# Scores ahead of transposes, logits ahead of low parts: a new order inside the head-pair loop of a one-core hybrid attention layer

## Chip, cores and metric

One core of one Trainium2 chip runs the whole layer in one launch. The metric is the device time of that launch in microseconds (us); lower is better. The engines are named as in the profile: PE (TensorE, with PEld for its weight loads), DVE (VectorE), ACT (ScalarE), POOL (GpSimd) and SP (SyncE, which here only issues DMAs). They run separate instruction queues, each in its own written order, and meet through semaphores.

## What is computed

One decoder layer for a sequence of 256 tokens and a model width of 1024, in float32. The input is RMS-normed and projected to two head groups of 8 heads with 64 columns each. Group A is attention with forget gates: a bias of cumulated log gates is added to the causal logits. Group B is block-sparse attention with a distance bias; with 256 tokens there is one block, so it is plain causal attention with that bias. Every head's output is multiplied by a SiLU gate; the 16 heads' outputs are projected back to 1024 columns, RMS-normed and added to the input.

```python
h = rms_norm(x, norm_pre_g)
q_a, k_a, v_a, g_a, f_a, q_b, k_b, v_b, g_b = split(h @ w_in)
logits_a = q_a @ k_a.T / 8 + F[t] - F[s]          # F = cumsum(log_sigmoid(f_a + b)), causal
logits_b = q_b @ k_b.T / 8 - slope * (t - s)       # causal
y_a = softmax(logits_a) @ v_a * silu(g_a)
y_b = softmax(logits_b) @ v_b * silu(g_b)
out = x + rms_norm(concat(y_a, y_b) @ w_out, norm_post_g)
```

## The kernel before

Every float32 product is made of parts. A matrix is split into a high part (ACT copies it to a rounded type) and a low part (DVE subtracts the high part from the original), and a product is three matmuls: high by high, low by high, high by low.

The weights come in units of 128 x 1024 floats. SP loads them one after the other into a ring of four slots (`raw`); ACT makes the high part of a unit (line 369), DVE the low part (line 570, `next_low`), and the slot is free for the next load when the low part is done. Units of values and gates come first. From unit `QK_0` on, units alternate: `query_unit(i)`, `key_unit(i)` for the head pairs i = 0 to 7 (pairs 0 to 3 are group A, 4 to 7 group B), and behind them the second half of the output weights.

The attention part is a loop written out by hand, with one head pair in each of several stages. In turn i (i = 2 to 7) PE runs `query(i)` and `key(i)`, 24 matmuls each at line 850, `scores(i - 1)` at line 944, `transposes(i - 2)` of the probabilities at lines 951 to 953 and `values(i - 2)` at lines 961 to 966. The other engines do in a turn, in the order of their queues:

- ACT: high part of query i (482); high parts of the transposed probabilities of i-2 (457, 458); high part of the weights of key i+1 (369); high part of y of i-3 (471, from turn 3 on); the four exponentials of i-1 with their row sums (465); high part of key i (486); high part of the weights of query i+2 (369); the upper half of the value result of i-2, `y_cross` (477).
- DVE: `query_low(i)` (719); `probs_low(i - 2, 0)` and `(i - 2, 1)` (695), the low parts of the transposed probabilities, with `row_logits(i - 1)` (709), four reductions that add the bias and find the row maximum, between them; the low part of the weights of key i+1 (570); `row_inverses(i - 1)` (715); `key_low(i)` (724); the low part of the weights of query i+2 (570); `gated(i - 2)` (730, 735), which sums y and multiplies it with its gate.
- POOL: `norm_probs(i - 1)`, two multiplications of the probabilities by the inverse row sums (324); the bias of pair i, two operations (310 and 311 for group A, 318 for group B); the low part of y of i-2 (330).

What waits for what, where the change touches it: `scores(i - 1)` needs the high and low parts of query and key i-1, and that `row_logits(i - 2)` has read the bank. `transposes(i - 2)` needs `norm_probs(i - 2)`. `row_logits(i - 1)` needs the scores and both bias operations of pair i-1. `values(i - 2)` needs both `probs_low(i - 2, ...)`. `query(i)` and `key(i)` need the low part of their weights. The bias operations of pair i wait for `row_logits(i - 1)`.

Ahead of the loop DVE also makes the low parts of the weights of `key_unit(2)` and `query_unit(3)`. Behind it comes a tail in which PE fills its waits with the first parts of the output projection (`out_part`, line 1011): out parts, `transposes(6)`, `scores(7)`, out parts, `values(6)`, out parts, `transposes(7)`, out parts, `values(7)`, and the rest of the projection. In the tail ACT's queue holds the high part of y of pair 5 ahead of the high parts of the transposed probabilities of pair 6, and DVE's holds `gated(5)`, `probs_low(6, 0)`, `row_logits(7)`, `probs_low(6, 1)`. The change does not touch the tail's order.

Of the kernel before, what the change touches and what calls it, by code (L numbers as in the profile page):

```python
# [62 lines left out]
def hybrid_layer(nc, xt, x, g_pre, w_units, w_f, f_bias, w_out, g_post, out):  # L63
# [5 lines left out]
    def sem(name):  # L69
        return ctx.enter_context(nc.semaphore(name))  # L70

    with ctx:
# [103 lines left out]
        s_logits = sem("logits_ready")  # L176
# [382 lines left out]
        def _(dve):  # L559
# [8 lines left out]
            def unit_low(s, count, width=UNIT):  # L568
                dve.wait_ge(s_hi, count)
                nc.vector.tensor_tensor(w[1][:, s, 0:width], raw[:, s, 0:width], w[0][:, s, 0:width].bitcast(F32),  # L570
                                        ALU.subtract).then_inc(s_lo, 1)
# [120 lines left out]
            def probs_low(i, n):  # L692
                dst, src = ((p_t0, pt0_ps), (p_t1, pt1_ps))[n]
                dve.wait_ge(s_pthi, 2 * i + n + 1)
                nc.vector.tensor_tensor(dst[1][:, :, :], src, dst[0][:, :, :].bitcast(F32),  # L695
                                        ALU.subtract).then_inc(s_ptlo, 1)

            def row_logits(i):
                dve.wait_ge(s_qk, i + 1)
                dve.wait_ge(s_bias, 2 * i + 2)  # L700
                for a in range(2):
                    if i < FOX_PAIRS:
                        biases = bias[:, a, 0:P], decay[:, 2 * i + a, :]
                    else:
                        biases = bias[:, a, P:SEQ], bias[:, a, :]
                    for t, (lo, hi) in enumerate(((0, P), (P, NB))):
                        c = 2 * a + t

                        nc.vector.tensor_tensor_reduce(out=logits[:, a, lo:hi], in0=s_ps[a][:, lo:hi], in1=biases[t],  # L709
                                                       scale=-SCALE, scalar=3.0e38, op0=ALU.add, op1=ALU.min,  # L710
                                                       accum_out=neg_max[:, c:c + 1]).then_inc(s_logits, 1)

            def row_inverses(i):
                dve.wait_ge(s_exp, 4 * i + 4)
                nc.vector.reciprocal(row_inv[:, :], row_sum[:, :]).then_inc(s_inv, 1)  # L715

            def query_low(i, b):
                dve.wait_ge(s_qhi, i + 1)
                nc.vector.tensor_tensor(q[1][:, b, :], bank[0][:, 0:SEQ], q[0][:, b, :].bitcast(F32),
                                        ALU.subtract).then_inc(s_qlo, 1)  # L720
# [16 lines left out]
            def next_low(u):  # L737

                unit_low(u % RING, u + 1)

            def query_unit(i):

                return QK_0 + 2 * i

            def key_unit(i):

                return QK_0 + 2 * i + 1
# [11 lines left out]
            row_inverses(0)  # L759
            key_low(1)  # L760
            next_low(key_unit(2))
            next_low(query_unit(3))

            dve.wait_ge(s_gate, 1)
            for i in range(2, PAIRS):
                if i > 2:
                    dve.wait_ge(s_norm, 2 * i - 2)
                query_low(i, i % 2)
                probs_low(i - 2, 0)
                row_logits(i - 1)  # L770
                probs_low(i - 2, 1)
                next_low(key_unit(i + 1))
                row_inverses(i - 1)
                key_low(i)
                next_low(query_unit(i + 2))
                gated(i - 2)
# [64 lines left out]
        def _(pe):  # L841
# [94 lines left out]
            def scores(i, b):  # L936
                pe.wait_ge(s_qhi, i + 1)
                pe.wait_ge(s_qlo, i + 1)
                pe.wait_ge(s_khi, i + 1)
                pe.wait_ge(s_klo, i + 1)  # L940
                for t, (lo, hi) in enumerate(((0, P), (P, NB))):
                    for n, (x, z) in enumerate(PASSES):
                        for a, own in enumerate(head_rows):
                            last = nc.tensor.matmul(s_ps[a][:, lo:hi], q[x][own, b, t * P:(t + 1) * P],  # L944
                                                    k[z][own, 0:hi - lo], start=n == 0, stop=n == len(PASSES) - 1)
                last.then_inc(s_qk, 1)
# [22 lines left out]
            def query(i, b, halfway=None):  # L969
                pe.wait_ge(s_lo, QK_0 + 1 + 2 * i)  # L970
                column_unit(bank[0], 2 * b, h, halfway)

            def key(i, b):
                pe.wait_ge(s_lo, QK_0 + 2 + 2 * i)
                column_unit(bank[1], 2 * b + 1, h)
# [11 lines left out]
            def attend(i, b, first=False):  # L987
                pe.wait_ge(s_qlo, i)
                query(i, b)
                if not first:  # L990
                    pe.wait_ge(s_ptlo, 2 * i - 4)
                transposes(i - 2)
                pe.wait_ge(s_logits, 4 * i - 4)
                scores(i - 1, 1 - b)
                key(i, b)
                if not first:
                    pe.wait_ge(s_ysum, 2 * i - 4)
                values(i - 2)
# [93 lines left out]
```

## Time and profile before

| | |
|---|---|
| Median of 3 runs | 147.05 us (146.78 to 147.18) |
| The profiled execution: time, span | 147.58 us, 145.8 us |
| PE matmul busy | 137.5 us, 94% |
| PEld busy | 129.0 us, 88% |
| DVE busy | 110.8 us, 76% |
| ACT busy | 99.6 us, 68% |
| POOL busy | 44.7 us, 31% |
| Granted TensorE clock, mean over the span | 0.992 |

The time of the profiled execution holds 1.78 us outside its span. All times of the trace count from the start of the span. The loop runs from 63.4 us (first matmul of `query(2)`) to 112.97 us, the tail from there on. A row of the timeline gives start and duration; durations of neighbours on one engine overlap a little, so the distance between two starts is what an instruction takes from its engine. "x2" in a row of PE's scores means the two heads of the pair, which use different halves of the array's rows.

### The profile page before, as it was taken

Reading aid. Unit: us, or ns where it says so; the run is one execution under the profiler, and the core shown is the slowest. Engines: PE = TensorE matmul, PEld = TensorE weight load, DVE = VectorE, ACT = ScalarE, POOL = GpSimd, SP = SyncE. Lnnn points to the kernel's source line nnn. Section 1 sums busy time; section 2 is a strip of 40 time slices with the busy share of each in tenths; the row PEclk is TensorE's granted clock in tenths of the full one; section 3 lists DMA queues with packets and bytes.
Section 4 is the critical chain, followed back from the end, with each engine's and each line's share of the span. In section 5 each row is a group of like instructions: output and inputs, shape, how many; then the busy total and the mean of one; then the engine's idle time right before and its main releaser. Section 6 shows DMA issues by size and latency. Waiting matters only on the chain.

```text
span 145.8 us, 2904 instructions
## 1 busy us (share of the span) xinstructions
PE 137.5 (94%) x1076; PEld 129.0 (88%) x1076; DVE 110.8 (76%) x243; ACT 99.6 (68%) x209; POOL 44.7 (31%) x70
## 2 busy tenths in 40 slices
PE   7999999999999999999999999999999999999920
PEld 7899899999999999998899999999999888898910
DVE  0384965999999996679989898989899866240891
ACT  4466989488957488598568788795959495244530
POOL 2621100000000012019293755465472924200241
PEclk9999999999999999999999999999999999999996
DMA  4899997488876999941744443525174000000034
GB/s 90 268 323 396 400 389 296 127 334 241 288 214 216 323 378 406 368 161 18 270 148 144 146 144 103 189 66 216 27 246 173 0 0 4 0 0 0 0 144 144
DMA packets 9725, 26.96 MB, mean 185 GB/s; under 512 B 1384, under 2 KB 2416, under 8 KB 9456
## 3 DMA queue, kind: packets, MB, share of 16 engines
q1 hardware_dynamic: 9120, 25.57, 50.7%
q10 hardware_dynamic: 592, 1.22, 2.5%
q8 instruction: 8, 0.13, 0.4%
q14 instruction: 5, 0.04, 0.1%
HBM read 25.73 MB, written 1.06 MB: 184 GB/s over the span
## 4 chain that ended last, share of the span: by engine, by line
PE 43%; DVE 24%; DMA 15%; ACT 6%; issue 4%; SPq 3%; POOL 2%; POOLq 1%; ACTq 0%; DVEq 0%
PE bank L850 20%; PE bank L1011 13%; DVE w_lo L570 11%; DMA h<-in_x 6%; DMA raw_out<-in_w_out 5%; DMA raw<-in_w_units 4%; PE bank L944 4%; DVE h L614 2%; DVE v L628 2%; DVE gate L635 2%; SPq L207 2%; DVE h_lo L641 2%; DVE wo_lo L646 2%; PE bank L961 1%; ACT w_hi L369 1%
## 5 line engine op out<-in xcount | busy, mean ns | idle before, releaser
L570 DVE TENSOR_TENSOR w_lo<-raw,w_hi 128x1024 fp32r<-128x1024 f32 (+1 forms) x33 | 44.2, 1343 | 8.4 <-ACT w_hi L369 8.4
L369 ACT ACTIVATE w_hi<-raw 128x1024 fp32r<-128x1024 f32 (+1 forms) x33 | 34.5, 1057 | 6.4 <-DMA raw<-in_w_units 4.6
L850 PE MATMUL bank<-h_hi,w_hi 128*128 128x256 f32 x128 | 36.7, 286 | 0.0
L850 PE MATMUL bank<-h_hi,w_lo 128*128 128x256 f32 x128 | 35.6, 278 | 0.0
L850 PE MATMUL bank<-h_lo,w_hi 128*128 128x256 f32 x128 | 35.6, 278 | 0.0
L850 PEld LDWEIGHTS bank<-h_hi,w_hi 128*128 128x128 f32 x128 | 24.1, 188 | 0.9
L850 PEld LDWEIGHTS bank<-h_hi,w_lo 128*128 128x128 f32 x128 | 24.0, 188 | 0.0
L850 PEld LDWEIGHTS bank<-h_lo,w_hi 128*128 128x128 f32 x128 | 24.0, 188 | 0.0
L324 POOL TENSOR_TENSOR probs<-probs,row_inv 128x256 f32<-128x256 f32 (+1 forms) x16 | 12.9, 828 | 23.0 <-DVE row_inv L715 23.0
L850 PE MATMUL bank<-xg_hi,w_hi 128*128 128x256 f32 x64 | 17.9, 280 | 0.0
L310 POOL TENSOR_TENSOR bias<-squares,causal 128x256 f32<-128x256 f32 x4 | 6.2, 1548 | 37.7 <-DMA squares<-decay_rows_scratch 37.7
L850 PE MATMUL bank<-xg_lo,w_hi 128*128 128x256 f32 x64 | 17.7, 277 | 0.0
L850 PE MATMUL bank<-xg_hi,w_lo 128*128 128x256 f32 x64 | 17.7, 276 | 0.0
L465 ACT ACTIVATE probs<-logits,neg_max 128x128 f32<-128x128 f32 (+1 forms) x32 | 14.2, 447 | 2.4 <-DVE neg_max L709 2.3
L850 PEld LDWEIGHTS bank<-xg_hi,w_hi 128*128 128x128 f32 x64 | 12.0, 188 | 0.1
L850 PEld LDWEIGHTS bank<-xg_lo,w_hi 128*128 128x128 f32 x64 | 12.0, 188 | 0.0
L850 PEld LDWEIGHTS bank<-xg_hi,w_lo 128*128 128x128 f32 x64 | 12.0, 188 | 0.0
L695 DVE TENSOR_TENSOR p_t_lo<-bank,p_t_hi 128x512 fp32r<-128x512 f32 (+1 forms) x16 | 8.7, 550 | 3.2 <-ACT p_t_hi L457 3.0
L860 PE MATMUL bank<-w_hi,xg_hi 128*128 128x256 f32 (+2 forms) x50 | 10.4, 330 | 0.3 <-ACT w_hi L400 0.3
L860 PE MATMUL bank<-w_hi,xg_lo 128*128 128x256 f32 (+2 forms) x50 | 9.9, 320 | 0.0
L860 PE MATMUL bank<-w_lo,xg_hi 128*128 128x256 f32 (+2 forms) x50 | 9.9, 319 | 0.0
L730 DVE TENSOR_TENSOR y_sum<-bank,y_cross 64x256 f32<-64x256 f32 x16 | 6.6, 413 | 3.7 <-ACT y_cross L477 3.4
(131 smaller groups left out, 318.5 us busy)
## 6 DMA issues: line engine op xcount, KB each, us to landing
raw<-in_w_units SPq DMA_DIRECT2D x30, 512.0 KB, 5.4
raw_out<-in_w_out SPq DMA_DIRECT2D x4, 512.0 KB, 6.6
raw<-in_w_out SPq DMA_DIRECT2D x4, 512.0 KB, 3.4
h<-in_x SPq DMA_DIRECT2D x2, 512.0 KB, 8.0
squares<-decay_rows_scratch ACTq DMA_DIRECT2D x1, 1024.0 KB, 7.9
x_t<-in_x SPq DMA_DIRECT2D x1, 1024.0 KB, 7.6
raw<-in_w_units SPq DMA_DIRECT2D x3, 256.0 KB, 4.8
out<-x_t SPq DMA_DIRECT2D x3, 256.0 KB, 2.0
```

Source lines behind the costliest of these rows:

```text
L207: sp.dma_start(raw[:, u % RING, lo:hi].rearrange("p (a c) -> p a c", a=n), w_units[units, :, part][0:n].rearrange("a p c -> p a c")).then_ ...
L310: pool.tensor_tensor(bias[:, :, 0:P], decay[:, heads, 0:P], mask, ALU.add).then_inc(s_bias, 1)
L324: pool.tensor_tensor(probs[:, :, lo:hi], probs[:, :, lo:hi], row_inv[:, t::2].unsqueeze(2).to_broadcast((P, 2, hi - lo)), ALU.mult).then_i ...
L369: nc.scalar.activation(w[0][:, s, 0:width], raw[:, s, 0:width], ACT.Copy).then_inc(s_hi, 1)
L465: nc.scalar.activation(probs[:, a, lo:hi], logits[:, a, lo:hi], ACT.Exp, bias=neg_max[:, c:c + 1], scale=-1.0, accum_out=row_sum[:, c:c + ...
L570: nc.vector.tensor_tensor(w[1][:, s, 0:width], raw[:, s, 0:width], w[0][:, s, 0:width].bitcast(F32), ALU.subtract).then_inc(s_lo, 1)
L695: nc.vector.tensor_tensor(dst[1][:, :, :], src, dst[0][:, :, :].bitcast(F32), ALU.subtract).then_inc(s_ptlo, 1)
L730: nc.vector.tensor_tensor(y_sum[own, :], pv_ps[head_rows[0], a, :], y_cross[own, :], ALU.add).then_inc(s_ysum, 1)
L850: last = nc.tensor.matmul(dst, stationary(a, j), moving(b, j), start=n == 1, stop=n == count * len(PASSES))
L860: last = nc.tensor.matmul(v_banks[t][c][:, lo - first:hi - first], xg[a][:, u, t * P:(t + 1) * P], w[b][:, u % RING, lo:hi], start=u == 0 ...
L944: last = nc.tensor.matmul(s_ps[a][:, lo:hi], q[x][own, b, t * P:(t + 1) * P], k[z][own, 0:hi - lo], start=n == 0, stop=n == len(PASSES) - 1)
L1011: last = nc.tensor.matmul(dst, y[a][:, p, t * P:(t + 1) * P], wide, start=p == 0 and (a, b) == PASSES[0], stop=p == PAIRS - 1 and (a, b) = ...
```

## The change

Two queues get another order. On PE, each turn of the loop runs query, scores, transposes, key, values; before, the transposes stood ahead of the scores. On DVE, each turn runs `row_logits(i - 1)` ahead of `probs_low(i - 2, 0)`, no longer between the two `probs_low`. And the low part of the weights of `query_unit(3)`, which stood ahead of the loop, is made in turn 2, behind `probs_low(0, 1)` and ahead of the low part of `key_unit(3)`. No instruction is added or removed, and the queues of ACT, POOL and SP are as before.

```diff
             key_low(1)
             next_low(key_unit(2))
-            next_low(query_unit(3))
 
             dve.wait_ge(s_gate, 1)
             for i in range(2, PAIRS):
                 if i > 2:
                     dve.wait_ge(s_norm, 2 * i - 2)
                 query_low(i, i % 2)
+                row_logits(i - 1)
                 probs_low(i - 2, 0)
-                row_logits(i - 1)
                 probs_low(i - 2, 1)
+                if i == 2:
+                    next_low(query_unit(3))
                 next_low(key_unit(i + 1))
                 row_inverses(i - 1)
                 key_low(i)
...
             def attend(i, b, first=False):
                 pe.wait_ge(s_qlo, i)
                 query(i, b)
+                pe.wait_ge(s_logits, 4 * i - 4)
+                scores(i - 1, 1 - b)
                 if not first:
                     pe.wait_ge(s_ptlo, 2 * i - 4)
                 transposes(i - 2)
-                pe.wait_ge(s_logits, 4 * i - 4)
-                scores(i - 1, 1 - b)
                 key(i, b)
```

## Rows read from the trace of the kernel before

**Rows 1.** Chain that ended last, in order of time (start, us, what).

```profile
67.68 1.75 DVE w_lo L570
```

**Rows 2.** Timeline of PE, turn 2 and its end (start, us, instruction, count, idle before).

```profile
66.24 0.28 PE L850 MATMUL bank<-h_hi,w_lo 128*128 128x256 f32 x1
66.73 0.33 PE L951 MATMUL bank<-ident,probs 128*128 128x128 f32 x1 [0.21 <-POOL probs L324]
...
67.33 0.27 PE L953 MATMUL bank<-ident,probs 128*128 128x128 f32 x1
67.53 0.33 PE L944 MATMUL bank<-k_hi,q_hi 64*128 64x128 f32 x2
...
68.21 0.28 PE L944 MATMUL bank<-k_hi,q_lo 64*128 64x256 f32 x2
68.42 0.39 PE L850 MATMUL bank<-h_hi,w_hi 128*128 128x256 f32 x1
...
71.23 0.28 PE L850 MATMUL bank<-h_hi,w_lo 128*128 128x256 f32 x1
71.85 0.39 PE L961 MATMUL bank<-p_t_hi,v 128*128 128x256 f32 x1 [0.34 <-DVE p_t_lo L695]
...
72.67 0.33 PE L850 MATMUL bank<-h_hi,w_hi 128*128 128x256 f32 x1
```

**Rows 3.** Timeline of PE: the first matmul of `values(1)`, `(5)` and `(6)`.

```profile
80.01 0.28 PE L961 MATMUL bank<-p_t_hi,v 128*128 128x256 f32 x1
...
112.25 0.28 PE L961 MATMUL bank<-p_t_hi,v 128*128 128x256 f32 x1
...
120.30 0.28 PE L961 MATMUL bank<-p_t_hi,v 128*128 128x256 f32 x1
```

**Rows 4.** Timeline of DVE, tail.

```profile
119.57 0.42 DVE L695 TENSOR_TENSOR p_t_lo<-bank,p_t_hi 128x256 fp32r<-128x256 f32 x1
```

**Rows 5.** Timeline of DVE, turn 2.

```profile
65.96 1.80 DVE L570 TENSOR_TENSOR w_lo<-raw,w_hi 128x1024 fp32r<-128x1024 f32 x1 [0.53 <-ACT w_hi L369]
...
69.35 0.41 DVE L719 TENSOR_TENSOR q_lo<-bank,q_hi 128x256 fp32r<-128x256 f32 x1
69.68 0.67 DVE L695 TENSOR_TENSOR p_t_lo<-bank,p_t_hi 128x512 fp32r<-128x512 f32 x1
70.28 0.28 DVE L709 CUSTOM_DVE_ANT_0 logits<-bank,bias 128x128 f32<-128x128 f32 x1
...
71.39 0.41 DVE L695 TENSOR_TENSOR p_t_lo<-bank,p_t_hi 128x256 fp32r<-128x256 f32 x1
71.72 1.21 DVE L570 TENSOR_TENSOR w_lo<-raw,w_hi 128x1024 fp32r<-128x1024 f32 x1
...
73.11 0.42 DVE L724 TENSOR_TENSOR k_lo<-bank,k_hi 128x256 fp32r<-128x256 f32 x1
```

**Rows 6.** Timeline of ACT, turn 7 and the start of the tail.

```profile
108.55 0.60 ACT L457 ACTIVATE p_t_hi<-bank 128x512 fp32r<-128x512 f32 x1 [0.27 <-PE bank L953]
...
112.73 1.05 ACT L369 ACTIVATE w_hi<-raw 128x1024 fp32r<-128x1024 f32 x1
...
116.79 0.42 ACT L471 ACTIVATE xg_hi<-y 128x256 fp32r<-128x256 f32 x1 [2.19 <-DVE y L735]
```

**Rows 7.** Timeline of POOL, turns 2 and 3.

```profile
66.63 1.71 POOL L310 TENSOR_TENSOR bias<-squares,causal 128x256 f32<-128x256 f32 x1
68.31 1.72 POOL L311 TENSOR_TENSOR squares<-squares,causal 128x256 f32<-128x256 f32 x1
73.10 1.61 POOL L324 TENSOR_TENSOR probs<-probs,row_inv 128x256 f32<-128x256 f32 x2 [3.07 <-DVE row_inv L715]
74.67 1.71 POOL L310 TENSOR_TENSOR bias<-squares,causal 128x256 f32<-128x256 f32 x1
76.34 0.74 POOL L311 TENSOR_TENSOR squares<-squares,causal 128x256 f32<-128x256 f32 x1
```

**Rows 8.** The page's sixth part: loads of weight units (KB each, median us to landing).

```profile
raw<-in_w_units SPq DMA_DIRECT2D x30, 512.0 KB, 5.4
```

## The prediction

> **What bounds the kernel now.** I read the page first: PE's matmuls are busy 94% of the span, no other engine over 76% (the table of the profile above). That says PE, but a share over the whole span does not say what a reordering is worth. So I went to the chain of work that ended last. From the values of turn 2 (71.85) to the end of the projection it is PE alone; ahead of that it runs for some us through DVE, and the low part of `query_unit(3)`, 1.75 us, is its largest piece there [rows 1]. Then PE's timeline shows what turn 2 loses. Matmuls of 256 columns follow each other every 0.11 to 0.12 us. Two gaps are wider: 66.24 to 66.73, where the transposes wait for POOL's normed probabilities (0.38 lost), and 71.23 to 71.85, where the values wait for DVE (0.50 lost) [rows 2]. A matmul behind a wait is also longer, 0.33 for 0.27 and 0.39 for 0.28: its weight load is not hidden, 0.06 and 0.11. Together 1.05 us. From turn 3 on PE never waits: `values(1)` at 80.01 and `values(5)` at 112.25 lie four times 8.06 apart [rows 3].
>
> The reader should see one thing more, which the chain does not show: how near behind PE the others run. In the tail `probs_low(6, 1)` starts at 119.57 and takes 0.42 [rows 4]; with the 0.05 that lay between such an end and PE in turn 2 (71.39 + 0.41 to 71.85) `values(6)` could have started at 120.04, and it started at 120.30 [rows 2, 3, 5]. The slack is 0.26 us. What makes `probs_low(6, 1)` so late is a relay: transposes(5), ACT from the transposed probabilities (108.55) to the weights (112.73) and, past DVE's `gated(5)`, to y (116.79) [rows 6], then `probs_high(6)`, DVE's low part, logits, low part.
>
> **Part 1, PE's order.** In turn 2 the scores fill the wait. `scores(1)` starts 0.20 behind the query's last matmul, as it does behind the transposes (67.33 to 67.53), at 66.44; it lasts 0.68 to its last start (67.12). The transposes then start at 67.33 if this step costs what scores to key cost, 0.21, and the last of them at 67.93 (before at 67.33, with the scores still to come). The key follows at 68.04 instead of 68.42 [rows 2]. Its first load would be hidden again (0.11). A gain of 0.49 for PE here.
>
> In every other turn no wait is filled and five steps between blocks are only dealt out anew: query to transposes (0.11), transposes to scores (0.20), scores to key (0.21 + 0.11) become query to scores (0.20), scores to transposes, transposes to key (0.11 by the nearest case, matmuls that follow each other). Scores to transposes the trace does not show. From below it is 0.11, a plain step; from above 0.32, as scores to key with the exposed load. I take 0.27, with the 0.06 that a transpose showed behind a wait: PE's turn changes by -0.05, next to nothing. With the ends it is -0.2 to 0 a turn.
>
> But in each turn the transposes come later, by the scores in front of them: 0.20 - 0.11 + 0.68 + 0.27 = 1.04 us.
>
> **Part 2, DVE's order and the moved low part.** `query_low(2)` no longer stands behind `query_unit(3)` and starts at 67.68 instead of 69.35. `row_logits(1)` follows at 68.02, but it needs the bias of pair 1. POOL's two operations took 1.71 and 1.72 us; the same at 76.34 took 0.74 [rows 7]. The long ones each start just before a DVE subtraction of a unit: DVE's own, issued at 65.96, takes 1.80 where one beside an idle POOL takes 1.21 [rows 5]. They take turns. DVE has the first turn until 67.68, POOL's first operation runs to 68.31, and the second, with DVE's subtraction gone, ends at 68.31 + 0.74 = 69.05. So logits start at 69.08, 1.06 late, and DVE stands. They take 1.11 (70.28 to 71.39), `probs_low(0, 0)` 0.60, `(0, 1)` 0.42: `values(0)` at 71.25, not 71.85 [rows 2, 5].
>
> The Trainium skill says of this, in "SBUF — State Buffer", section "SBUF: two separate sides", that VectorE with two SBUF inputs and GpSimd hold a shared port pair for a whole instruction and the other blocks; these rows agree. By a split of bandwidth instead, the split norms of the next paragraph would cost POOL some 0.5 us less and the sum would be about 0.2 lower.
>
> Now the moved subtraction is late in its turn: 71.13 to 72.34 (1.21), and `query(3)` needs it: 72.38 against 72.67 before, while PE would be ready at 71.25 + 0.82 = 72.07. Of 1.05 us in reach 0.29 are left. Behind it `key_unit(3)` takes 1.14; `key_low(2)` and `norm_probs(1)` start at 73.5 to 73.65, not at 73.1 [rows 5, 7]. And the low part of `query_unit(4)` now is issued 0.34 behind `key_low(2)`, while POOL is in the first of its two norm operations (1.61 for both), since ACT, which waited for logits before, has the high part ready. DVE gets the pair between the two: the second norm ends at about 76.1 to 76.3, and `transposes(1)`, ready at 76.15, wait up to 0.2. The biases of pair 2 end at about 77.8 to 78.1 instead of 77.08. `row_logits(2)` waits for them, and with 1.11 + 0.60 + 0.42 + 0.05 `values(1)` starts at 80.0 to 80.3. It was 80.01: the gain is gone. I take +0.1.
>
> **Part 3, the loop.** From ACT's start on the transposed probabilities to its query weights is 4.18, to the end of DVE's gated y another 4.06, then query low 0.33, logits 1.11, low parts 0.60 and 0.47: next turn's values at 10.75 us [rows 2, 5, 6]. PE used to need 3.7 from ACT's start (108.55) to the values of that turn (112.25) [rows 3, 6]; without the scores between them, 1.04, it needs 2.66, and comes to the next ones at 2.66 + 8.06 = 10.7, where it used to come 1.04 later. So cover of a microsecond is used up, and PE meets DVE at each values: 0 to 0.1 a turn, taken as 0, with the 0.05 that PE's turn gains against it.
>
> **Part 4, the tail.** Here the order is the old one, so PE comes to `values(6)` as early as before, but the relay started with `transposes(5)`, 1.04 later. `values(6)` starts at 120.04 + 1.04 + 0.1 = 121.2 and shows its load (0.11); before 120.30. That is 0.99, and behind `values(6)` only PE works until the projection ends, so it stays to the end.
>
> **DMAs.** The moved low part frees the slot for `query_unit(5)` 3 us later; ACT wants that unit two turns on, at about 81, and a load takes 5.4 us from issue to landing [rows 8]. It is hidden; without that cover it would be a load's length late.
>
> **Sum.** +1.0 us. The profiled execution becomes 148.6 from 147.58; it lay 0.53 above the median, so the median goes from 147.05 to **148.05**.
>
> **Rivals.**
> *A, faster: only PE counts.* All 1.05 us of waits go and the relay has room: 146.0. For it: PE is the whole chain from 71.85. Against it: 0.26 us of slack at `values(6)`. It decides if the relay shrinks by 0.8.
> *B, same: the front gain stays.* If POOL's second bias ends by 68.3 and the norms are not split, `query(3)` starts at 71.6 and `values(1)` about 0.9 earlier; the tail takes it back: 147.1. Against it: POOL cannot start that bias before 68.31 and needs 0.74.
> *C, slower still.* If scores to transposes costs 0.32 and the key's load is exposed too (0.11), PE loses 0.12 a turn; if DVE and POOL collide in the group B turns as well, 0.1 to 0.2 more each: 148.8.
>
> **Numbers.** Forecast (+0.45 to +1.5) 0.62, A 0.07, B 0.17, C 0.14. The bounds: steps -0.4, turn 2 from -0.5 to +0.3, loop up to +0.5. With B's half inside, the range is 147.1 to 148.8. A difference under 0.3% (0.44 us) cannot be told from none. Faster 0.07, same 0.17, slower 0.76.
>
> **What would show it.** After: scores at 66.4 with no gap; logits(1) at 69.1 with DVE idle ahead of it; `query(3)` at 72.4; POOL's second norm of pair 1 or its bias at about 1.7 to 2 us; `values(1)` at 80.0 to 80.3; turns of 8.05 to 8.15; and in the tail PE waiting 0.5 to 1 us for DVE at `values(6)`, near 121.2. If PE does not wait there, the forecast is wrong.

## The result, and the profile after

The median of 21 runs is 148.42 us (147.74 to 150.20), against 147.18 us for the kernel before (21 runs, 146.35 to 149.31). Now and then an execution of either kernel is slower as a whole, and the ratio leaves those out. It is 1.0081, with an interval of 1.0054 to 1.0108: the change costs 0.8%, or 1.19 us on 147.18. Forecast were 148.05 us and a difference of +1.0.

The profiled execution took 147.79 us, for a span of 146.0 us at a granted clock of 0.993. The page's table of engines, after:

```profile
PE 136.9 (94%) x1076; PEld 128.0 (88%) x1076; DVE 112.7 (77%) x243; ACT 99.1 (68%) x209; POOL 44.8 (31%) x70
```

As many instructions, and nearly the busy times of the table before the change. DVE alone has 1.9 us more, although it does the same work; nearly all of it, 1.8 us, is in the low parts of the weights (46.0 for 44.2), which run longer where POOL holds them up. The time is in the order, so the timelines have to tell it.

PE's timeline from the end of the query to the first values (start, us, instruction):

```profile
66.12 0.28 PE L851 MATMUL bank<-h_hi,w_lo 128*128 128x256 f32 x1
66.33 0.33 PE L945 MATMUL bank<-k_hi,q_hi 64*128 64x128 f32 x2
...
67.00 0.28 PE L945 MATMUL bank<-k_hi,q_lo 64*128 64x256 f32 x2
67.21 0.33 PE L952 MATMUL bank<-ident,probs 128*128 128x128 f32 x1
...
67.81 0.27 PE L954 MATMUL bank<-ident,probs 128*128 128x128 f32 x1
67.84 0.36 PE L851 MATMUL bank<-h_hi,w_hi 128*128 128x256 f32 x1
68.04 0.28 PE L851 MATMUL bank<-h_lo,w_hi 128*128 128x256 f32 x1
...
70.75 0.28 PE L962 MATMUL bank<-p_t_hi,v 128*128 128x256 f32 x1
```

The scores come 0.21 behind the query, with no gap, and both waits of turn 2 [rows 2] are gone: `values(0)` stands at 70.75, not at 71.85. The new step from scores to transposes is 0.21, with 0.06 of exposed load on the first transpose (0.33 for 0.27).

DVE's timeline in turns 2 and 3 (in brackets the idle time before, and what ended it):

```profile
66.92 0.42 DVE L719 TENSOR_TENSOR q_lo<-bank,q_hi 128x256 fp32r<-128x256 f32 x1 [0.61 <-ACT q_hi L482]
67.73 0.29 DVE L709 CUSTOM_DVE_ANT_0 logits<-bank,bias 128x128 f32<-128x128 f32 x1 [0.39 <-POOL squares L311]
...
72.94 2.06 DVE L570 TENSOR_TENSOR w_lo<-raw,w_hi 128x1024 fp32r<-128x1024 f32 x1 [0.41 <-ACT w_hi L369]
```

And POOL's:

```profile
63.62 1.61 POOL L324 TENSOR_TENSOR probs<-probs,row_inv 128x256 f32<-128x256 f32 x2 [9.74 <-DVE row_inv L715]
65.18 1.72 POOL L310 TENSOR_TENSOR bias<-squares,causal 128x256 f32<-128x256 f32 x1
66.86 0.73 POOL L311 TENSOR_TENSOR squares<-squares,causal 128x256 f32<-128x256 f32 x1
72.30 1.61 POOL L324 TENSOR_TENSOR probs<-probs,row_inv 128x256 f32<-128x256 f32 x2 [4.71 <-DVE row_inv L715]
```

As forecast, the second bias operation shrinks from 1.72 [rows 7] to 0.73 once DVE's subtraction is out of its way, and DVE stands ahead of the logits until that bias is there. But it stands 0.39 us, not 1.06. In turn 3 the norms of pair 1 are not split (1.61 for both); instead DVE's low part of `query_unit(4)`, 72.94, waits behind the second one and takes 2.06, where the same instruction took 1.74 before (at 74.06) and one beside an idle POOL takes 1.21 [rows 5]. `values(1)` is the first to feel it.

The later values of PE's timeline, and the tail:

```profile
79.08 0.36 PE L962 MATMUL bank<-p_t_hi,v 128*128 128x256 f32 x1 [0.15 <-DVE p_t_lo L695]
...
117.96 0.40 PE L1012 MATMUL bank<-wo_hi,xg_lo 128*128 128x512 f32 x1
118.41 0.47 PE L1012 MATMUL bank<-w_hi,xg_hi 128*128 128x512 f32 x1
118.72 0.40 PE L1012 MATMUL bank<-w_lo,xg_hi 128*128 128x512 f32 x1
...
119.64 0.40 PE L1012 MATMUL bank<-w_hi,xg_lo 128*128 128x512 f32 x1
120.37 0.36 PE L962 MATMUL bank<-p_t_hi,v 128*128 128x256 f32 x1 [0.34 <-DVE p_t_lo L695]
```

And what DVE does in front of it:

```profile
119.80 0.42 DVE L695 TENSOR_TENSOR p_t_lo<-bank,p_t_hi 128x256 fp32r<-128x256 f32 x1
```

`values(5)` is at 111.47, so from there to `values(6)` it is 8.90 us; before it was 8.05 [rows 3]. Two places on PE hold the 0.85. Matmuls of the projection follow each other every 0.23 us. The step from 117.96 to 118.41 is 0.45 and the next 0.31: 0.30 lost to the low part of y of pair 5, which POOL makes from 117.51 to 118.26. From 119.64 to 120.37 it is 0.73: 0.50 lost to `probs_low(6, 1)`. The rest, 0.05, is the turn itself. The two losses have not two causes, though: nothing that DVE does for `probs_low(6, 1)` waits for the out part of pair 5, so without the first pause PE would only have waited longer at `values(6)`.

One thing misleads in this pair of profiles: the spans differ by 0.2 us (145.8 and 146.0), the medians by 1.2. The place is ahead of the loop, in ACT's timeline, where the fourth unit of the output weights is awaited. First before, then after:

```profile
60.20 1.06 ACT L373 ACTIVATE wo_hi<-raw_out 128x1024 fp32r<-128x1024 f32 x1 [1.49 <-DMA raw_out<-in_w_out]
```
```profile
58.46 1.06 ACT L373 ACTIVATE wo_hi<-raw_out 128x1024 fp32r<-128x1024 f32 x1 [0.15 <-DMA raw_out<-in_w_out]
```

That load was late in the profiled execution of before. DVE takes the low part of this unit ahead of the inverse row sums of pair 0, and POOL's norms wait for those. They started at 63.62 after, and before at

```profile
65.06 1.61 POOL L324 TENSOR_TENSOR probs<-probs,row_inv 128x256 f32<-128x256 f32 x2 [9.35 <-DVE row_inv L715]
```

The experiments below had to find out whether the waits of turn 2 come from this.

### The profile page after: what moved, and what is told of

Its sections match the earlier page's. It is cut to its first block, busy times and chain, and to the rows that moved or that the text cites. A ratio compares the mean times of both kernels' runs of the same rounds, so it can differ in the third digit from the quotient of the medians.

```text
span 146.0 us, 2904 instructions
## 1 busy us (share of the span) xinstructions
PE 136.9 (94%) x1076; PEld 128.0 (88%) x1076; DVE 112.7 (77%) x243; ACT 99.1 (68%) x209; POOL 44.8 (31%) x70
## 3 DMA queue, kind: packets, MB, share of 16 engines
q10 hardware_dynamic: 592, 1.22, 2.2%
HBM read 25.73 MB, written 1.06 MB: 184 GB/s over the span
## 4 chain that ended last, share of the span: by engine, by line
PE 67%; DVE 9%; POOL 7%; ACT 7%; issue 4%; DMA 3%; SPq 1%; POOLq 1%; DVEq 0%
PE bank L851 34%; PE bank L861 15%; PE bank L1012 9%; DMA raw<-in_w_units 3%; DVE w_lo L570 3%; ACT probs L465 2%; PE bank L945 2%; DVE logits L709 2%; POOL bias L310 2%; POOL probs L324 2%; DVE p_t_lo L695 2%; PE bank L962 1%; ACT w_hi L369 1%; PE bank L952 1%; POOL x_t L355 1%
## 5 line engine op out<-in xcount | busy, mean ns | idle before, releaser
L570 DVE TENSOR_TENSOR w_lo<-raw,w_hi 128x1024 fp32r<-128x1024 f32 (+1 forms) x33 | 46.0, 1398 | 7.4 <-ACT w_hi L369 7.3
L861 PE MATMUL bank<-w_hi,xg_hi 128*128 128x256 f32 (+2 forms) x50 | 9.9, 319 | 1.1 <-ACT w_hi L400 1.1
L457 ACT ACTIVATE p_t_hi<-bank 128x512 fp32r<-128x512 f32 x8 | 4.8, 598 | 8.6 <-PE bank L954 8.6
L695 DVE TENSOR_TENSOR p_t_lo<-bank,p_t_hi 128x512 fp32r<-128x512 f32 (+1 forms) x16 | 8.2, 547 | 3.0 <-ACT p_t_hi L457 3.0
```

Of the source, the lines that this page charges most:

```text
L457: nc.scalar.activation(p_t0[0][:, :, :], pt0_ps, ACT.Copy).then_inc(s_pthi, 1)
L861: last = nc.tensor.matmul(v_banks[t][c][:, lo - first:hi - first], xg[a][:, u, t * P:(t + 1) * P], w[b][:, u % RING, lo:hi], start=u == 0 ...
```

## The experiments

Each ratio is to the kernel before, run on the same chip in the same rounds. Stage distances are between first matmuls of `values(i)`, written V(i), in the profiled execution:

| kernel | ratio (interval) | V0 | V0 to V1 | V1 to V5 | V5 to V6 | V0 to V7 |
|---|---|---|---|---|---|---|
| before | 1 | 71.85 | 8.16 | 32.24 | 8.05 | 55.37 |
| before, again | 1.0023 (0.9989 to 1.0057) | 71.89 | 8.17 | 32.23 | 8.05 | 55.41 |
| before, third slot | 0.9996 (0.9966 to 1.0026) | 70.86 | 8.07 | 32.23 | 8.05 | 55.27 |
| after | 1.0081 (1.0054 to 1.0108) | 70.75 | 8.33 | 32.39 | 8.90 | 56.65 |
| after, again | 1.0104 (1.0043 to 1.0164) | 70.85 | 8.33 | 32.39 | 8.88 | 56.63 |
| after, third slot | 1.0071 (1.0037 to 1.0106) | 71.06 | 8.33 | 32.38 | 8.91 | 56.65 |
| last turn in the old order | 1.0041 (1.0006 to 1.0076) | 70.98 | 8.32 | 32.39 | 8.43 | 56.12 |
| ACT's tail swapped | 1.0068 (1.0036 to 1.0100) | 71.00 | 8.93 | 32.39 | 8.37 | 56.65 |
| both of these | 1.0066 (1.0024 to 1.0107) | 70.85 | 8.32 | 32.39 | 8.42 | 56.07 |
| change in turn 2 only | 1.0010 (0.9980 to 1.0039) | 71.29 | 8.32 | 32.32 | 8.04 | 55.61 |
| PE's order only | 1.0162 (1.0111 to 1.0213) | 70.97 | 8.40 | 33.52 | 8.69 | 57.64 |
| DVE's order only | 1.0066 (1.0036 to 1.0097) | 71.22 | 9.09 | 32.23 | 8.04 | 56.34 |
| moved low part only | 1.0045 (1.0009 to 1.0081) | 70.95 | 8.82 | 32.24 | 8.05 | 56.02 |
| the same with a wait | 1.0031 (0.9992 to 1.0070) | 71.33 | 8.64 | 32.32 | 8.05 | 55.92 |

### The kernel before, again

No edit. Expected:

> The kernel before, unchanged, for a second profile of it and for the noise of a comparison. Theory (relay): in the profile of the changed kernel ACT and DVE entered the loop 1.4 us earlier than in the profile of before (first norm operation of POOL at 63.62 against 65.06), because a load of output weights landed earlier. If that differs from execution to execution, this profile can show the transposes of turn 2 without a wait, values(0) at 70.6 to 70.9 instead of 71.85, values(5) at 110.9 to 111.2, and a span near 144.8. Rival (the waits of turn 2 belong to the order of the queues): values(0) again at 71.8 to 71.9 and the span at 145.8. Time: no difference, ratio 1.000 within 0.3%.

The ratio is no different from 1, but the profiled execution had the late load again: ACT had the unit at 60.23, the norms of pair 0 started at 65.09, V(0) was at 71.89, the span 145.8. The hoped-for early execution did not come, and the question stayed open.

### A third slot for the output weights

On the kernel before: one more slot, and the fourth unit's load issued one place earlier in SP's queue, so that it lands earlier.

```diff
-OUT_BEHIND = (V_UNITS + 3, V_UNITS + 5, V_UNITS + 11, V_UNITS + 13)
+OUT_BEHIND = (V_UNITS + 3, V_UNITS + 5, V_UNITS + 11, V_UNITS + 12)
...
-        raw_out = sb("raw_out", [P, 2, UNIT])
+        raw_out = sb("raw_out", [P, 3, UNIT])
...
-                if j > 1:
-                    sp.wait_ge(s_olo, j - 1)
-                sp.dma_start(raw_out[:, j % 2, :], w_out[j]).then_inc(s_raw_out_in[j % 2], 16)
+                if j > 2:
+                    sp.wait_ge(s_olo, j - 2)
+                sp.dma_start(raw_out[:, j % 3, :], w_out[j]).then_inc(s_raw_out_in[j % 3], 16)
...
```

> The kernel before with a third staging slot for the output weights and the load of output unit 3 issued one unit load earlier; both queues in the old order. Theory: the waits of turn 2 (1.05 us in two profiles of before) come from the high part of output unit 3, for which ACT waits 1.5 us at 60.2; with an earlier landing ACT and DVE enter turn 2 over 1 us earlier, the transposes of turn 2 and values(0) do not wait, and the span is 144.8 to 145.0: ratio 0.993 to 0.998 (some executions of before are early as they are). Rival (the waits belong to the order of DVE's queue): values(0) still at 71.8, ratio 1.000.

The span is 144.7, as expected, and PE waits for nothing in the loop or in the tail. ACT's row for the unit, and PE's first matmuls of `values(0)` and `values(6)`:

```profile
58.27 1.05 ACT L373 ACTIVATE wo_hi<-raw_out 128x1024 fp32r<-128x1024 f32 x1
```
```profile
70.86 0.28 PE L961 MATMUL bank<-p_t_hi,v 128*128 128x256 f32 x1
...
119.21 0.28 PE L961 MATMUL bank<-p_t_hi,v 128*128 128x256 f32 x1
```

So the load's landing is what makes the waits of turn 2. But the ratio is 1.00, not the 0.993 to 0.998 expected. This execution took 146.52 us, and the median of before beside it was 146.65: by its time, the usual execution of before is already one without these waits, and the two profiles of before happened to be late ones. That is read from the times; no profile of the unchanged kernel before shows an early landing. With this kernel as the measure, span 144.7 against 146.0, the profiles show +1.3 us, which answers to the 1.19 of the ratio: 0.26 in turn 3 (V0 to V1), 0.16 in the four turns behind it, 0.85 from `values(5)` to `(6)`, 0.11 from there to `values(7)` (the exposed load of `values(6)` for the most part), less 0.11 by which V(0) comes earlier.

### The third slot on the kernel after, and the kernel after again

The same diff, on the kernel after:

> The changed kernel with the third staging slot and the earlier load of output unit 3, which took the waits of turn 2 out of the kernel before (span 144.7). Theory: in the change PE has no wait left in turn 2 that the landing could set, and the loss is in turn 3, the loop and the tail: values(0) at 70.7 to 70.9, values(5) to values(6) at 8.9, span 146.0, so 1.3 us over the kernel before with the same staging and ratio 1.006 to 1.009 to before. Rival (the change's loss comes with the late landing): ratio under 1.003.

And the kernel after without an edit:

> The changed kernel once more, on the chip and in the call of its repaired versions. Theory: ratio 1.007 to 1.010; a second profile, with values(5) to values(6) again at 8.9 us; if the output weights land late in it, values(0) to values(1) is near 8.9 instead of 8.33, by the norms of pair 1 being split (2.60 us) and logits(2) waiting 1 us for the bias. Rival (the first profile is not typical): a tail distance near 8.05.

Both repeat the kernel after within 0.02 us in each stage (8.33, 32.38 and 32.39, 8.91 and 8.88). With the third slot the loop as a whole began 0.3 us later (norms of pair 0 at 63.93), so V(0) and the span of 146.3 lie a little above what was expected; the ratio of the kernel after again, 1.0104 from six runs, lies a little above its 1.010. The load was early in all three, so the loss does not need a late one. What a late one adds, the swapped kernel below shows. The median of the first, 148.01, lies 1.47 above the 146.54 of the third slot on before, from another chip.

### The last turn in the old order

On the kernel after, PE runs turn 7 as before, so that `transposes(5)` are as early as they were.

```diff
                 query(i, b)
-                pe.wait_ge(s_logits, 4 * i - 4)
-                scores(i - 1, 1 - b)
+                if i < PAIRS - 1:
+                    pe.wait_ge(s_logits, 4 * i - 4)
+                    scores(i - 1, 1 - b)
...
                 transposes(i - 2)
+                if not (i < PAIRS - 1):
+                    pe.wait_ge(s_logits, 4 * i - 4)
+                    scores(i - 1, 1 - b)
                 key(i, b)
```

> The changed kernel, with PE's old order (transposes ahead of scores) in the last turn of the loop alone, turn 7. Theory (relay): the cost sits between values(5) and values(6), where the chain transposes(5), ACT, gated y, ACT, low parts, values(6) starts 1.04 us later than before. With transposes(5) early again that distance falls from 8.90 to about 8.5 us, since DVE still comes later from the turns before, and the time is 0.4 us (0.2 to 0.8) under the changed kernel: ratio to before 1.003 to 1.007. Rival 1 (each turn's steps on PE cost more in the new order): one turn of six is restored, so a sixth of 1.2 us, 0.2 us, and the distance values(5) to values(6) stays 8.9. Rival 2 (the loss is in turn 2): no change, 1.008.

V5 to V6 falls from 8.90 to 8.43, and the whole from 1.0081 to 1.0041, as expected (the two intervals overlap, so it is the stage that tells). The high part of y of pair 5 starts at 116.33, not 117.02. PE waits neither at the out part of pair 5 (118.52 to 118.75) nor at `values(6)` (119.89 to 120.12): with `transposes(5)` early the relay costs nothing, so the late transposes do drive the tail. The 0.38 that stays is no rest of it. Most of it is a new wait, 0.29 at `transposes(6)`, which the last repair below explains.

### ACT's tail swapped

On the kernel after, ACT takes the transposed probabilities of pair 6 ahead of y of pair 5.

```diff
-            y_high(PAIRS - 3)
             probs_high(PAIRS - 2)
+            y_high(PAIRS - 3)
```

> The changed kernel, with one exchange in ACT's tail: the high parts of the transposed probabilities of pair 6 are made ahead of the high part of y of pair 5, not behind it. The loop is untouched. Theory (relay): ACT waits 2.35 us for y there while the transposes have been done since 115.9; without that wait DVE is bound by its own queue, PE waits less at values(6), and the time falls by 0.5 us (0.3 to 0.9) against the changed kernel: ratio to before 1.002 to 1.006; values(5) to values(6) near 8.5 us or less. Rival 1 (cost of PE's steps or of the loop): the tail's order does not matter, ratio stays 1.008 and the distance from values(0) to values(5) stays 40.7.

V5 to V6 is 8.37: `values(6)` no longer waits for DVE, and what is left, 0.27, is lost at the out part of pair 5, which waits for POOL's low part of y (118.33 to 119.08; the matmul starts at 119.23). The ratio, expected at 1.002 to 1.006, is 1.0068 (1.0036 to 1.0100); that interval holds both the 0.5 us that the stage gained and no gain at all. The profile cannot explain the median of twelve runs, but it shows something else: this execution had the load late (59.74, not quite the 60.20 of before), and with it turn 3 cost 8.93. It is the one profile of a changed kernel in which the forecast's own premise held, so it shows what the forecast described. DVE's timeline:

```profile
73.44 1.55 DVE L570 TENSOR_TENSOR w_lo<-raw,w_hi 128x1024 fp32r<-128x1024 f32 x1
...
77.65 0.29 DVE L709 CUSTOM_DVE_ANT_0 logits<-bank,bias 128x128 f32<-128x128 f32 x1 [1.10 <-POOL squares L311]
```

POOL's and PE's:

```profile
73.29 2.60 POOL L324 TENSOR_TENSOR probs<-probs,row_inv 128x256 f32<-128x256 f32 x2 [4.71 <-DVE row_inv L715]
```
```profile
72.13 0.36 PE L851 MATMUL bank<-h_hi,w_hi 128*128 128x256 f32 x1 [0.26 <-DVE w_lo L570]
```

`query(3)` waits for the moved low part, until 72.13; DVE's subtraction is issued 0.15 behind the start of the first norm and comes between the two, which then take 2.60 for 1.61; the biases are late, DVE stands 1.10 ahead of the logits, and `values(1)` is at 79.93.

### Both repairs together

```diff
-            y_high(PAIRS - 3)
             probs_high(PAIRS - 2)
+            y_high(PAIRS - 3)
...
+                if i < PAIRS - 1:
+                    pe.wait_ge(s_logits, 4 * i - 4)
+                    scores(i - 1, 1 - b)
```

> The changed kernel with both repairs of the tail at once: PE's old order in turn 7, and ACT's high parts of the transposed probabilities of pair 6 ahead of the high part of y of pair 5. Theory (relay): each repair alone left about 0.35 of the 0.85 us between values(5) and values(6) (8.43 and 8.37, from 8.90; 8.05 before), because after the one the other still delayed; with both the distance is 8.05 to 8.10 and PE does not wait at values(6). Left are turn 3 and the loop, 0.3 to 0.6 us: ratio 1.002 to 1.004. Rival (a third cause in the tail, DVE's own lateness): 8.3 or more stays.

Missed. V5 to V6 is 8.42, no better than with either alone, and the ratio 1.0066. `values(6)` follows the projection without a gap (119.75 to 119.98). Another wait is there, at `transposes(6)`:

```profile
114.92 0.40 PE L1016 MATMUL bank<-wo_hi,xg_lo 128*128 128x512 f32 x1
115.45 0.30 PE L952 MATMUL bank<-ident,probs 128*128 128x128 f32 x1
```
```profile
112.71 2.60 POOL L324 TENSOR_TENSOR probs<-probs,row_inv 128x256 f32<-128x256 f32 x2 [1.93 <-DVE row_inv L715]
```
```profile
113.11 1.30 DVE L570 TENSOR_TENSOR w_lo<-raw,w_hi 128x1024 fp32r<-128x1024 f32 x1 [0.17 <-ACT w_hi L369]
```

The norms of pair 6 are split by a DVE subtraction issued 0.40 behind their start. In the kernel before with the third slot they start at 111.66, the subtraction at 112.73, 1.07 behind, and they take 1.61. The kernel with the last turn alone in the old order has the same split (112.84, 2.60) and the same late `transposes(6)` (115.06 to 115.58). The kernel after has neither: there the norms start at 112.96, the subtraction comes at 113.89, 0.93 behind, the norms take 1.61 and `transposes(6)` follow the projection in step (114.83 to 115.07). So this wait was not hidden under the others; the old order in the last turn makes it. In the kernel after the tail has two chains: DVE's low part, which alone sets the 0.85, and behind it POOL's low part of y, worth 0.27 when the first is gone. The expectation took what the old last turn had left for the second chain; it was this new wait.

### The change in turn 2 only

On the kernel before: PE's new order and the logits ahead of both low parts at i = 2, and the moved low part; the other turns as before.

```diff
-            next_low(query_unit(3))
...
                 query_low(i, i % 2)
+                if i == 2:
+                    row_logits(i - 1)
                 probs_low(i - 2, 0)
-                row_logits(i - 1)
+                if i > 2:
+                    row_logits(i - 1)
                 probs_low(i - 2, 1)
+                if i == 2:
+                    next_low(query_unit(3))
...
+                if first:
+                    pe.wait_ge(s_logits, 4 * i - 4)
+                    scores(i - 1, 1 - b)
                 if not first:
                     pe.wait_ge(s_ptlo, 2 * i - 4)
                 transposes(i - 2)
-                pe.wait_ge(s_logits, 4 * i - 4)
-                scores(i - 1, 1 - b)
+                if not (first):
+                    pe.wait_ge(s_logits, 4 * i - 4)
+                    scores(i - 1, 1 - b)
```

> The change in turn 2 alone: scores ahead of transposes on PE, logits ahead of the low parts on DVE, and the low part of query unit 3 moved into turn 2; turns 3 to 7 in the old order on both engines. Theory (relay): the later turns and the tail are as before, values(5) to values(6) is 8.05 us again, and what stays is turn 2 by itself: little gain where ACT and DVE come late, 0.3 us lost where they come early (query(3) waits for the moved low part). Ratio 1.000 to 1.003. Rival 2 (the loss of the change is in turn 2): 1.006 to 1.008.

1.0010, not told from 1. The turn behind it keeps its 8.32, and V5 to V6 is 8.04: the tail's loss needs the new order in the later turns. Its own profile has the load early, with no wait for this version to win; what it does in a late execution was not seen.

### PE's order only

```diff
                 query(i, b)
+                pe.wait_ge(s_logits, 4 * i - 4)
+                scores(i - 1, 1 - b)
                 if not first:
                     pe.wait_ge(s_ptlo, 2 * i - 4)
                 transposes(i - 2)
-                pe.wait_ge(s_logits, 4 * i - 4)
-                scores(i - 1, 1 - b)
                 key(i, b)
```

> PE's new order alone (scores ahead of transposes in every turn); DVE as before: low parts, logits between them, query unit 3 ahead of the loop. Theory (relay, and DVE's order): the transposes come 1.04 us later in each turn, and DVE, which takes the first low part ahead of the logits, cannot use the earlier scores; so logits and exponentials come later and every turn is bound by that loop: 8.2 to 8.3 us from values to values where the change has 8.10, and the time is 1.5 to 2.5 us over before, ratio 1.010 to 1.017. Rival (the cost is in PE's steps alone): as the change, 1.008, with turns of 8.10.

1.0162, the dearest of all: a turn takes 8.38 (33.52 over four), a little over the 8.2 to 8.3 expected. With the transposes 1 us later, ACT's and DVE's work on them ends behind PE's key in every turn. `values(2)` shows it: its first matmul is 0.39 behind the last of the key (87.38 to 87.77) and takes 0.35. The new DVE order is what brings turns back to 8.10.

### DVE's order only

```diff
-            next_low(query_unit(3))
...
                 query_low(i, i % 2)
+                row_logits(i - 1)
                 probs_low(i - 2, 0)
-                row_logits(i - 1)
                 probs_low(i - 2, 1)
+                if i == 2:
+                    next_low(query_unit(3))
```

> The DVE half of the change alone: logits ahead of both low parts in every turn, the low part of query unit 3 moved into turn 2; PE in the old order. Theory (relay): transposes and scores come as before, PE's turns stay 8.06 and values(5) to values(6) 8.05; what is lost is in turns 2 and 3 only (logits wait for scores that stand behind the transposes, query(3) waits for the moved low part, the bias of pair 2 comes late): 0.5 to 0.9 us, ratio 1.003 to 1.006. Rival (DVE's order is the cost of the change and PE's is free): 1.008.

1.0066, a little over what was expected. Turns (8.06) and tail (8.04) cost nothing, and `query(3)` does not wait; all is in turn 3, 9.09, where the norms of pair 1 are split (72.97, 2.59), `transposes(1)` wait 0.83 for them, and the logits behind the scores 1.24.

### The moved low part only

```diff
-            next_low(query_unit(3))
...
                 probs_low(i - 2, 1)
+                if i == 2:
+                    next_low(query_unit(3))
```

> Only the low part of query unit 3 moved behind probs_low(0, 1) in turn 2; everything else as before. Theory: the wait at values(0) goes (0.5 us in an execution where the output weights land late), and query(3) waits for the moved low part instead; the two are near each other. Ratio 0.999 to 1.004, values(1) within 0.2 us of before in a late execution and 0.2 to 0.6 us late in an early one; turns 3 to 7 of 8.06. Rival (the late low part of query unit 3 was the only obstacle): ratio 0.993.

1.0045, where at most 1.004 was expected, and for another reason than expected: `query(3)` does not wait for the moved low part. Turn 3 costs 8.82, 0.75 more than the 8.07 of the third slot on before, and PE's wait names the cause. PE's, POOL's and DVE's timelines:

```profile
75.18 0.30 PE L952 MATMUL bank<-ident,probs 128*128 128x128 f32 x1 [0.57 <-POOL probs L324]
```
```profile
72.44 2.60 POOL L324 TENSOR_TENSOR probs<-probs,row_inv 128x256 f32<-128x256 f32 x2 [4.69 <-DVE row_inv L715]
```
```profile
72.59 1.55 DVE L570 TENSOR_TENSOR w_lo<-raw,w_hi 128x1024 fp32r<-128x1024 f32 x1
```

The row of POOL holds two multiplications that are not equal. Taken singly, they are

```profile
72.44 0.62 POOL L324 TENSOR_TENSOR probs<-probs,row_inv 128x256 f32<-128x256 f32 x1 [4.69 <-DVE row_inv L715]
73.01 2.02 POOL L324 TENSOR_TENSOR probs<-probs,row_inv 128x512 f32<-128x512 f32 x1
```

and in the kernel after the second of them is

```profile
72.87 1.04 POOL L324 TENSOR_TENSOR probs<-probs,row_inv 128x512 f32<-128x512 f32 x1
```

Here DVE's subtraction comes at 72.59, while the first multiplication runs, and the second then takes 2.02 for 1.04. In the kernel after it comes at 72.94, when the second has begun, and has to wait for that one to end.

### The same with a wait ahead of the low part of the weights of query i+2

DVE waits in turn 2 until both norms are done.

```diff
                 key_low(i)
+                if i == 2:
+                    dve.wait_ge(s_norm, 2 * i)
```

> The kernel in which only the low part of query unit 3 was moved, with one wait added on DVE in turn 2: the low part of query unit 4 waits until POOL has finished both norm operations of pair 1. No work moves. Without the wait that subtraction started at 72.59 between the two norm operations, which took 2.60 us for both instead of 1.61, and transposes(1) on PE waited 0.6 us. Theory (DVE and POOL hold something exclusively for a whole instruction, and POOL's second norm was locked out): the norms take 1.61 us again, PE does not wait at transposes(1), values(0) to values(1) falls from 8.82 to 8.1 to 8.3, and the kernel is 0.4 to 0.7 us faster although an engine waits more: ratio 0.999 to 1.002. Rival (they share bandwidth, or the norms were slow for another reason): the added wait costs or does nothing, ratio 1.0045 or more.

The norms are back at 1.61 and `transposes(1)` wait no more, though DVE does the same work later:

```profile
72.82 1.61 POOL L324 TENSOR_TENSOR probs<-probs,row_inv 128x256 f32<-128x256 f32 x2 [4.70 <-DVE row_inv L715]
74.39 0.73 POOL L310 TENSOR_TENSOR bias<-squares,causal 128x256 f32<-128x256 f32 x1
75.08 1.72 POOL L311 TENSOR_TENSOR squares<-squares,causal 128x256 f32<-128x256 f32 x1
```
```profile
74.47 1.73 DVE L570 TENSOR_TENSOR w_lo<-raw,w_hi 128x1024 fp32r<-128x1024 f32 x1 [1.42 <-POOL probs L324]
```

That is the split shown: one wait, no other edit, and 2.60 is 1.61. The size was missed: turn 3 is 8.64, not 8.1 to 8.3, and the ratio of 1.0031 is not told from the 1.0045 without the wait. DVE stood 1.42 us for the wait, collided with the biases instead, and now `values(1)` waits 0.41 for DVE.

## Why the prediction was right

The total, its sign and the tail were right. The way through turns 2 and 3 was right for an execution like the one it was read from, which by the medians is not the usual one; that the total held in spite of it is in part luck.

**Part 1, PE's steps: right.** Scores behind the query 0.21 (taken 0.20), scores to transposes 0.21 and 0.06 of load (taken 0.27 in all), transposes to key 0.03 from the last transpose and 0.20 to the key's second matmul, 0.23 where two plain steps make 0.22. Turns came out at 8.10 (8.05 to 8.15 forecast), 0.04 above those of before, where PE's own steps were to save 0.05. The relay of Part 3, forecast at 0 to 0.1 a turn and taken as 0, is part of it and adds 0.16 over four turns: `values(3)`, at 95.27, starts 0.19 behind the key's last matmul where 0.12 is plain, and shows its load (0.35 for 0.28).

**Part 2, turn 2: right in mechanism; the size goes with the landing of one load.** The step that failed is "the logits start at 69.08, 1.06 late": it took ACT, DVE and POOL as late against PE as the profiled execution showed them. In the profile after, DVE idles 0.39, `query(3)` waits for nothing, the norms of pair 1 stay together, and turn 3 loses 0.26 through DVE's low part of `query_unit(4)`, which waits behind the second norm instead of coming between. The moved low part is the start of that too: against the kernel before with the third slot, the inverse row sums stand at 72.05 for 71.47, the norms at 72.30 for 71.72, and the subtraction behind them ends at 75.00 for 74.42, 0.58 later each. In the swapped kernel's execution, with the load at 59.74, each step came near its place: idle 1.09, `query(3)` at 72.13 (72.38 forecast), norms split at 2.60, `values(1)` at 79.93 (80.0 to 80.3).

**Why the total held all the same.** The forecast measured from a late execution of before, in which turn 2 had lost 1.05 us, and let the change win that and lose it again. In an early execution neither happens: turns 2 and 3 together cost 0.15 there (0.26 less the 0.11 by which V(0) is earlier), for quite other reasons than the +0.1 of the forecast. That these two are alike is luck. What was left in both is the loop and the tail. Put together from two traces, a late execution after would have `values(6)` at 79.93 + 32.39 + 8.90 = 121.22, forecast 121.2 and 0.92 above [rows 3]; the early pair is 120.37 against 119.21, 1.16. The two differ by only 0.24.

**Part 4, the tail: right.** V5 to V6 was forecast to lengthen by 0.8 (`values(6)` from 120.30 to 121.2, less the 0.1 by which `values(5)` was to be later) and lengthened by 0.85, with PE standing at `values(6)` for DVE. The relay accounts for all of it. Counted from `values(5)`, `probs_low(6, 1)` ends 8.75 us on (111.47 to 120.22), and in the kernel before with the third slot 7.76 (111.16 to 118.92): 0.99 later, of 1.04 forecast. The slack was smaller than the 0.26 taken, since `values(6)` starts 0.15 behind that end and not 0.05: 119.21 - 118.92 - 0.15 = 0.14, and 0.99 - 0.14 is the 0.85. What the forecast did not have is the second chain, POOL's low part of y, which stops PE for 0.30 at the out part of pair 5, hidden under the first. The relay's start is confirmed: with `transposes(5)` early again, both of these waits are gone.

**The rivals.** A (only PE counts) is refuted: PE's own steps are as cheap as A needs and the time rose. B (the front gain stays) holds in its first half, the norms are not split and `query(3)` starts at 71.46; but by the medians the usual execution of before has no front loss to win back, and so the tail's loss stands alone. Set side by side, the two recorded profiles do what B says: `values(1)` is 0.93 earlier (79.08 for 80.01), the tail takes it back, and 147.79 us stand against 147.58. Only ACT's rows for the load, and the third slot, show that this was a late execution against an early one. C (the steps dear, 0.12 a turn): refuted by the 0.21 step and 8.10 turns.

**The port pair.** POOL's 1.72 against 0.73 and 2.60 against 1.61, in pairs that differ in what DVE issues, agree with the Trainium skill, "SBUF — State Buffer", section "SBUF: two separate sides", in that one instruction holds the pair whole and the other waits. The traces show the order too: a subtraction issued while POOL's first multiplication runs (0.15 to 0.41 us behind its start, five times) comes ahead of the second, and one issued when the second has begun (0.63 us and later, as in every other turn) waits for it to end.

Open: why the landing differs between executions (58.4 to 60.2 in ACT's row, third slots left out), and how often it is late, was not measured; only profiled executions show it.

## What to carry to other kernels

A wait in one profiled execution may belong to that execution: before a change is built on it, see whether a second profile has it, or remove its cause and look whether the median moves (here a third slot removed it, and the median did not move). When a stage with no wait of its own is moved later on the busiest engine, count the chains that start from it and the slack of each where they come back: here one chain set the loss of the tail and hid a second worth 0.3 us, and the order that mended the first moved a subtraction into POOL's norms, which gave a third. And a subtraction that nothing waits for yet can cost another engine's operations a microsecond, only by the moment at which it is issued.

## What the runs showed of the hardware

- Two POOL multiplications in a row, of 128 x 256 (0.62 us) and 128 x 512 (1.04), take 1.61 us alone, and 2.60 when a DVE subtraction of 128 x 1024 with both inputs in SBUF is issued 0.15 or 0.40 us behind the start of the first; the second then takes 2.02. Issued 0.64 behind (72.94, after), when the second has begun, DVE waits for its end: 2.06 us, and POOL keeps its 1.61. The subtraction alone takes 1.21 to 1.22.
- A POOL bias operation of 0.73 us takes 1.71 or 1.72 when such a subtraction is ahead of it.
- A load of 512 KB into the same slot, in kernels with the same code up to there, was there for ACT at 58.46 in one execution and at 60.23 in another. With a slot more and the load issued one place earlier, V(0) of the kernel before is at 70.86 for 71.85 and its span 144.7 for 145.8.
- A transpose behind scores that use half the array's rows starts 0.21 us behind the last of them; a 256-column matmul behind a transpose 0.03, and its successor 0.20.
